# Feed-forward begin: the input sums move between the first two pairs' taps, and three weight blocks are rounded earlier

## The reference

```python
def causal_dwconv(x, w, b):
    ...
    y = b
    for j in range(k):
        y = y + xp[:, j:j + s] * w[j]
    return y

def conv_ffn(h, w_up, conv_w, conv_b, w_down):
    u = causal_dwconv(h @ w_up, conv_w, conv_b)
    g, val = jnp.split(u, 2, axis=-1)
    return (jax.nn.silu(g) * val) @ w_down

h = h + conv_ffn(rms_norm(h, f_norm_g[layer]), f_w_up[layer], ...)
```

## Time and profile before

| | |
|---|---|
| median of 3 runs | 2260.4 us (2259.27 to 2263.41) |
| the profiled execution | 2255.15 us |
| its span | 2253.4 us |
| mean granted TensorE clock | 0.994 |
| busy: PE, PEld | 98%, 80% |
| busy: DVE, POOL, ACT | 63%, 50%, 43% |

### The profile page before, as it was taken

The page is one execution under the profiler, slowest core; times in us unless marked ns, Lnnn a source line. Parts: engine busy times, 40 slices in busy tenths (PEclk is TensorE's granted clock), DMA queues, the critical chain, the costliest instruction groups (busy, mean ns, idle before and its releaser), DMA issues. The chain is left out here.

```text
span 2253.4 us, 29138 instructions
## 1 busy us (share of the span) xinstructions
PE 2200.1 (98%) x10189; PEld 1802.5 (80%) x10189; DVE 1430.1 (63%) x2100; ACT 971.1 (43%) x1735; POOL 1137.4 (50%) x767
## 2 busy tenths in 40 slices
PE   9999999999999999999999999999999999999998
PEld 7786777888788888888888878878778888888886
DVE  6956565248866666787651115673797666669855
ACT  5535555224544544544431114451454544444443
POOL 2314334333677777655634332214257777765542
PEclk9999999999999999999999999999999999999999
DMA  5100000312123232674321110003023232248332
GB/s 184 47 19 1 1 0 29 122 38 80 71 89 122 89 122 89 207 250 114 98 103 56 47 47 29 26 34 119 19 89 122 89 116 95 104 153 296 102 98 94
DMA packets 66593, 203.36 MB, mean 90 GB/s; under 512 B 7392, under 2 KB 7520, under 8 KB 63392
## 3 DMA queue, kind: packets, MB, share of 16 engines
q1 hardware_dynamic: 63584, 187.19, 24.3%
q10 hardware_dynamic: 2880, 14.49, 1.7%
HBM read 152.89 MB, written 48.76 MB: 89 GB/s over the span
## 5 line engine op out<-in xcount | busy, mean ns | idle before, releaser
L596 POOL TENSOR_TENSOR whi<-stage,cons 128x1024 fp32r<-128x1024 f32 x60 | 117.9, 1964 | 540.9 <-PE ps L884 336.3
L882 PE MATMUL ps<-ahi,whi 128*128 128x512 f32 x896 | 368.0, 411 | 5.9 <-DVE alo L854 1.8
L884 PE MATMUL ps<-ahi,wlo 128*128 128x512 f32 x896 | 350.1, 391 | 0.0
L883 PE MATMUL ps<-alo,whi 128*128 128x512 f32 x896 | 349.8, 390 | 0.0
L674 POOL TENSOR_TENSOR wlo<-stage,whi 128x512 fp32r<-128x512 f32 x152 | 205.1, 1360 | 143.4 <-ACT whi L1135 143.4
L674 POOL TENSOR_TENSOR wlo<-A,whi 128x512 fp32r<-128x512 f32 x132 | 187.3, 1423 | 167.1 <-ACT whi L1147 167.1
L949 PE MATMUL ps<-ahi,whi 128*128 128x512 f32 x608 | 237.3, 390 | 4.5 <-ACT upv L1105 4.5
L1001 PE MATMUL ps<-x_hi,whi 128*128 128x512 f32 x616 | 240.7, 391 | 0.0
L1005 PE MATMUL ps<-x_hi,wlo 128*128 128x512 f32 x616 | 239.7, 389 | 0.0
L1003 PE MATMUL ps<-x_lo,whi 128*128 128x512 f32 x616 | 239.7, 389 | 0.0
L951 PE MATMUL ps<-alo,whi 128*128 128x512 f32 x608 | 237.2, 390 | 0.0
(11 more groups left out here) (338 smaller groups left out, 4657.0 us busy)
## 6 DMA issues: line engine op xcount, KB each, us to landing
stage<-in_wt SPq DMA_DIRECT2D x140, 512.0 KB, 4.1
hops<-hs SPq DMA_DIRECT2D x20, 1792.0 KB, 6.6
x_late<-hops SPq DMA_DIRECT2D x122, 256.0 KB, 2.7
A<-in_wt SPq DMA_DIRECT2D x88, 256.0 KB, 6.4
x_early<-hops SPq DMA_DIRECT2D x32, 256.0 KB, 5.1
hT<-in_xt SPq DMA_DIRECT2D x16, 256.0 KB, 6.6
hT<-in_xt ACTq DMA_DIRECT2D x8, 512.0 KB, 7.9
spill<-hT ACTq DMA_DIRECT2D x1, 4096.0 KB, 12.7
```

The costliest lines, as they stand in the source:

```text
L596: nc.gpsimd.tensor_tensor(whi[:, slot, :], stage[:, st, :], one_col.to_broadcast([P, 1024]), ALU.mult).then_inc(w_hi, 1)
L882: nc.tensor.matmul(bank, hi, rhs_k[0][:, tok], start=k_first, stop=False)
L883: nc.tensor.matmul(bank, hi, rhs_k[1][:, tok], start=False, stop=False)
L884: return nc.tensor.matmul(bank, lo, rhs_k[0][:, tok], start=False, stop=k_last)
```

## The change

Only the order of instructions on ACT and DVE changes, in both layers. No instruction is added or taken away, and PE, POOL and SP have the code of before.

On DVE, `sums(0)` now stands ahead of all taps, `sums(1)` between the gate taps and the value taps of pair 0, `sums(2)` with T3's first rest after the products of pair 0, and `sums(3)` with the next rest between the gate and the value taps of pair 1. After pair 1's products come the hidden differences and then the remaining rests. On ACT, the SiLU of pair 2 moves ahead of the copies of its value, weight block 2 ahead of the roundings of T1, and the T3 rounding of k = 1 moves from after pair 1 to after pair 0.

```diff
@@ -1199,37 +1199,54 @@
                 act.wait_ge(*counts(L, "down_read")(out_done_at(k, s)))
                 act_square(act, next_norm, pos, s, hT[:, k, :], sq)
 
-            for f in range(2):
+            def t2_hi(k):
+                act.wait_ge(sem("t_sum"), t_base(L) + 4 * k + 3)
+                round_piece(k, 3, rpieces[place(k, 5)][:, :])
+
+            def t1_hi(k):
+                act.wait_ge(sem("t_sum"), t_base(L) + 4 * k + 1)
+                round_piece(k, 4, ahi[:, k, halves[1]])
+
+            def t4_hi(k):
+                act.wait_ge(sem("t_lo"), t_count(L, "t1", k))
+                act.wait_ge(sem("t_sum"), t_base(L) + 4 * k + 4)
+                round_piece(k, 2, rpieces[place(k, 4)][:, :])
+
+            def gate_half(f):
                 evac(f, 0)
                 taps(f, 0)
+
+            def gate_silu(f):
                 for s in range(2):
                     silu(f, s)
-                evac(f, 1)
-                taps(f, 1)
-                for k in range(f, 2 * f + 1):
-                    t3_hi(k)
+
+            gate_half(0)
+            gate_silu(0)
+            evac(0, 1)
+            taps(0, 1)
+            for k in range(2):
+                t3_hi(k)
+            gate_half(1)
+            gate_silu(1)
+            evac(1, 1)
+            taps(1, 1)
+            t3_hi(2)
             for k in range(4):
-                act.wait_ge(sem("t_sum"), t_base(L) + 4 * k + 3)
-                round_piece(k, 3, rpieces[place(k, 5)][:, :])
+                t2_hi(k)
             t3_hi(3)
-            evac(2, 0)
-            taps(2, 0)
+            gate_half(PF - 1)
             act.wait_ge(w_used, t0 + PLAIN - 1)
             for n in range(2):
                 up_block(n)
-            evac(2, 1)
+            gate_silu(PF - 1)
+            evac(PF - 1, 1)
+            up_block(2)
             for k in range(4):
-                act.wait_ge(sem("t_sum"), t_base(L) + 4 * k + 1)
-                round_piece(k, 4, ahi[:, k, halves[1]])
-            for n in range(2, 4):
-                up_block(n)
-            for s in range(2):
-                silu(2, s)
-            taps(2, 1)
+                t1_hi(k)
+            up_block(3)
+            taps(PF - 1, 1)
             for k in range(4):
-                act.wait_ge(sem("t_lo"), t_count(L, "t1", k))
-                act.wait_ge(sem("t_sum"), t_base(L) + 4 * k + 4)
-                round_piece(k, 2, rpieces[place(k, 4)][:, :])
+                t4_hi(k)
             for i in range(SF):
                 up_step(i)
             operand_hi(3)
@@ -1422,27 +1439,30 @@
             for buf in (upg, upv):
                 nc.vector.memset(buf[:, 0:2], 0.0).then_inc(sem("zeroed"), 1)
 
-            for f in range(2):
-                both(f, 0)
-                if f == 1:
-                    sums(1)
-                both(f, 1)
-                for s in range(2):
-                    prod(f, s)
-                if f == 1:
-                    hidden_sums(0, range(4))
-                sums(2 * f)
-                t3_lo(f)
+            sums(0)
+            both(0, 0)
+            sums(1)
+            both(0, 1)
+            for s in range(2):
+                prod(0, s)
+            sums(2)
+            t3_lo(0)
+            both(1, 0)
             dve.wait_ge(w_used, t0 + 2)
             sums(3)
+            t3_lo(1)
+            both(1, 1)
+            for s in range(2):
+                prod(1, s)
+            hidden_sums(0, range(4))
             t3_lo(2)
             for k in range(4):
                 t2_lo(k)
             t3_lo(3)
-            both(2, 0)
+            both(PF - 1, 0)
             for k in range(4):
                 t1_lo(k)
-            both(2, 1)
+            both(PF - 1, 1)
             for k in range(4):
                 t4_lo(k)
             for i in range(SF):
```

## The result

The changed kernel takes 2266.61 us (median of 16 runs, 2262.34 to 2270.64), the kernel before, run beside it, 2257.82 us (16 runs, 2252.48 to 2263.41). The ratio is 1.0042, 95% interval 1.0033 to 1.0051: the change makes the kernel slower by about 9.5 us (7.4 to 11.5) by the ratio, 8.8 us by the two medians. The predicted time is met to 0.1 us. The predicted difference, +6.1, is not: the three runs that stood for the kernel before have a median 2.6 us above that of its sixteen runs, and this hid the rest.

What follows compares the result with a forecast made beforehand. PE, busy 98% of the span, bounds the kernel, with DVE's chain deciding product 5's start. Layer 0's +3.3 and layer 1's +2.8 gave +6.1 on 2260.4, so 2266.5 us; range for 8 in 10: 2257 to 2270.5.

Steps and rivals of the forecast that it cites:

- The predicted difference, +6.1: Whole kernel: product 5 later by 3.3 us in layer 0 and 2.8 in layer 1, +6.1 us in all.
- The direction and the path: DVE's chain to product 5, both layers: kernel slower, product 5 at 589.3 against 585.98 in layer 0.
- the walk in layer 0: DVE's operations priced one by one, from `sums(0)` at 520.3 to product 5 at 589.3.
- Filling the idle time and the meetings: DVE's sums fill 5.8 us of idle time, but meetings with POOL rise from 8.3 to 14.5 us.
- The faster rival: DVE: meetings cost little, gate taps of pair 2 start before 565.5; 2248.5 us, or 2254.5 for half; chance 0.15.
- The hidden write: SP's write of the first hidden blocks: issued at 562.0, lands at 568.7, gate taps of pair 2 1.35 late.
- ACT's order: ACT: SiLU of pair 2 ahead of T1's roundings; T1's rests leave DVE still for 2.7, product 0 gains 2.0.
- No change, by T4's rests alone: DVE's end of chain: T4's rests nearly alone, 2.5 instead of 6.3, pay for the 3.3; 2260 us, chance 0.25.
- The clock behind product 5: Slower rival on PE: clock falls behind product 5, 1.7 per layer, 3.4 in two layers; 2269.9 us, chance 0.1.
- one fall in four gaps before: PE's gaps in the kernel before: one of four followed by slow matmuls, taken for the clock fall's chance of 0.1.
- falls that lie under DVE's chain: PE in layer 1 before: the clock's 1.7 us lay under DVE's chain and does not count twice.
- The base: Starting time of the forecast: 2260.4 us, the median of three runs, 5.25 above the profiled execution of 2255.15.

Runs made afterwards that it cites:

- e6_quiet_new: Changed kernel with POOL's last three weight tiles before the Strassen part cut to 8 columns, both layers; 2256.19 us, ratio 0.9998 against the kernel before.
- e2_dve_old: Changed kernel with DVE's order of before; ACT's new order kept, except T3's rounding of k = 1; 2264.04 us, ratio 1.0034 against the kernel before.
- e1_act_old: Changed kernel with ACT's order of before, DVE's new order kept; 2258.09 us, ratio 1.0009 against the kernel before.
- e7_silu_late: Changed kernel with the two SiLUs of pair 2 moved back behind weight block 3 on ACT; 2257.73 us, ratio 1.0004 against the kernel before.
- e3_filled_gap: Changed kernel plus 16 unused matmuls between product 4 and the wait for product 5, both layers; 2261.18 us, ratio 1.0018 against the kernel before.
- e8_sums_wait: Changed kernel with POOL's sums of the first weight blocks held until DVE's four hidden differences are made; 2264.78 us, ratio 1.0042 against the kernel before.
- e5_quiet_old: Kernel before with POOL's last three weight tiles before the Strassen part cut to 8 columns, both layers; 2256.54 us, ratio 1.0003 against the kernel before.
- e4_interleaved: Same instructions reordered on DVE and ACT: sums between single taps, hidden differences, sums and rests alternating; 2244.70 us, ratio 0.9944 against the kernel before.
- e10_grouped: Interleaved order with one DVE stretch regrouped: four hidden differences, then seven sums, then three rests; 2251.61 us, ratio 0.9977 against the kernel before.

## Why the prediction was right, and where it was not

**The direction and the path.** Right. The forecast was slower, by product 5 in both layers, and the traces have it there. The times of the walk in layer 0, on the clock of the trace before (the changed kernel's `memset` lies 1.57 earlier): end of `sums(0)` 526.7 foretold, 526.7 found (525.13); gate taps of pair 2 at 568.8, found 568.9 (567.31); product 5 at 589.3, found 589.55 (587.98). In layer 1 +2.8 was foretold and +3.0 found. The terms of the sum, +6.1, came to +6.6.

**Filling the idle time and the meetings.** Right, with their prices: 2.27 and 2.77 beside a tile's rounding and split, about 1.7 and less for the hidden differences (6.22 for four against 6.3 in the walk). The faster rival asked for gate taps before 565.5 and fell; that its mechanism (no meetings, no loss) is the right counterpart is shown by e6_quiet_new. The Trainium skill, page "SBUF — State Buffer", section "Who interferes with whom", has DVE instructions with two SBUF inputs contend with POOL instructions that read SBUF, for ports that are an exclusive lock. The trace agrees for every group of sums, 0.69 alone and 2.27 to 2.78 beside a tile's rounding or split. The prediction adds "for a whole instruction", which that section says of DVE's 2-port modes; for these operations the rows show it.

**The hidden write.** Right to half a microsecond: 0.86 in layer 0, where 1.1 was the wait foretold (567.7 to 568.8), and none in layer 1.

**ACT's order.** Right, and by itself it was the heavier half (+7.7 us in e2_dve_old, +2.0 for DVE's order in e1_act_old): T1's rests waited 2.69 (foretold 2.7). The prediction called this one of several steps; e7_silu_late shows that with the SiLUs moved back product 5 would have come ahead of the old place.

**No change, by T4's rests alone.** Fell: 6.45, beside POOL's blocks, as foretold.

**The clock behind product 5.** This is the term that was mis-sized, by its chance. The prediction wrote that the clock might fall there, "3.4 in two layers", and gave that 0.1, after "one fall in four gaps before". It fell in both layers, for 2.3 + 1.6 = 3.9 us by the trace, and e3_filled_gap took it away again. The step that failed is the count of one in four: of the gaps before, the largest was 3.32. All gaps of 3.85 to 3.97 ahead of product 5 in these runs (the changed kernel, e1, e2, e7, e8, two layers each) were followed by 7 to 12 slow matmuls, ten of ten, those of 3.10 to 3.37 in three of five (the kernel before in layer 0, e5 and e6 in both layers). The forecast itself lengthened the gap ahead of product 5 from 3.48 to 4.2, counted from where the product could have started (4.12 was measured, 3.96 in the trace's bracket), longer than any that the count of one in four was taken from. And four gaps were too few for a chance: with the gaps ahead of the other products, those of 2.1 to 3.4 us in all these traces were followed by slow matmuls in nine cases of seventeen, one of them at 0.72 behind product 2 of the changed kernel's layer 1. That one cost nothing on product 5, as the prediction had it for falls that lie under DVE's chain. The Trainium skill, page "TensorE: Matmul & The Clock Gate", section "What's actually happening", has the clock follow how busy PE was recently; the runs agree with it as far as the filled gap of e3_filled_gap kept the clock at 1.00. Which of the gaps under 3.4 us are followed by a fall they don't tell.

**The base.** The absolute time came out right since two errors cancelled: the clock's 3.9 us left out, and 2.6 us too much in the median of three runs on which the forecast was put. A difference of two kernels is to be read from runs made side by side.

## What to carry to other kernels

Idle time of an engine is worth filling only if the work that moves there does not meet something dearer: look at what the neighbour on the same memory does at that moment, and take the price of a meeting from the trace. In an in-order queue, an instruction that waits for a late result (here a SiLU) must not stand ahead of work that another engine is waiting for. And a gap of TensorE is priced twice, as the gap and as the matmuls behind it at the lower clock, where nothing hides them.

## What the runs showed of the hardware that was not expected

In e4_interleaved and e10_grouped, who gets through in a meeting of DVE and POOL went with the way DVE's operations follow each other. Where each one needs the result of the one before (0.72 us from start to start), POOL gets in between, and DVE passes one operation per POOL operation: seven sums took 7.86 us in e10_grouped. Where two independent chains alternate (0.60 from start to start), DVE lost nothing over fourteen operations, and a POOL operation of 1.3 us took 4.79 in layer 0 of e4_interleaved and 3.67 in layer 1. What in the short pause lets POOL in was not tried. It is also not the whole rule: the six rests behind the hidden differences don't need each other, yet took 9.17 us beside POOL in e8_sums_wait, 8.07 in e6_quiet_new, and 3.70 for six without a meeting in e5_quiet_old. Each of them also waits for a rounding on ACT, but three such rests stood in e4_interleaved's alternating stretch and lost nothing, so what decides it stays open.

The clock after a gap is not decided by the gap's length alone: gaps of 3.31 us ahead of product 5 in the two layers of one execution (e5_quiet_old) were followed by no slow matmul in layer 0 and by thirteen, 2.8 us, in layer 1. Shorter gaps, ahead of product 0 in e2_dve_old, 2.11 and 2.36, were both followed by a fall (0.67 and 0.63), while 2.37 and 2.38 ahead of product 3 in e10_grouped were followed by none.
